# Pooling and embedding products from two-part operands in three passes, through the ring of weight slots

## What is computed

```
w in (2, 4, 8, 16):  pooled_g = window_sum_w(u_g) / min(t + 1, w) - u_g
a   = einsum("bsgc,gcd->bsgd", pooled, w_pool) * pool_scale
out = concatenate([a, gate_b * conv(gate_c * h_c)]) * silu(z)
h   = h + out @ w_out
```

```
gate = sigmoid(rmsnorm(h) @ w_ple_gate)
h    = h + (p @ w_ple_proj) * gate
```

## Time and profile before

| | |
|---|---|
| median of 3 runs | 3109.88 us |
| profiled execution's own time | 3109.86 us |
| its span | 3108.1 us |
| mean granted TensorE clock | 0.990 |
| TensorE busy | 97% |
| VectorE, ScalarE, GpSimd busy | 53%, 37%, 31% |
| 128x1024 high part, ScalarE | 279 times, mean 1058 ns |
| 128x1024 low part, GpSimd | 279 times, mean 2484 ns |

### The profile page before, as it was taken

The page is one execution under the profiler, slowest core; times in us unless marked ns, Lnnn a source line. Parts: engine busy times, 40 slices in busy tenths (PEclk is TensorE's granted clock), DMA queues, the critical chain, the costliest instruction groups (busy, mean ns, idle before and its releaser), DMA issues.

```text
span 3108.1 us, 38242 instructions
## 1 busy us (share of the span) xinstructions
PE 3014.0 (97%) x15412; PEld 2423.2 (78%) x15412; DVE 1649.9 (53%) x2710; ACT 1154.8 (37%) x1971; POOL 962.6 (31%) x700
## 2 busy tenths in 40 slices
PE   8999979999999999999999999999999999999998
PEld 7876658888878888777888866788778888888877
DVE  6989661025446564324234577767556655634436
ACT  3125553222341111113233276546445432333334
POOL 2210001232417786113531212321111133452522
PEclk9999989999999999999999999999999999999999
DMA  4110001112422333113342201331011155443323
GB/s 136 50 34 21 15 14 41 48 55 86 152 76 83 90 88 102 51 48 115 102 143 55 64 28 56 128 104 35 28 48 41 35 143 134 144 142 109 109 75 109
DMA packets 252658, 243.75 MB, mean 78 GB/s; under 512 B 15777, under 2 KB 198049, under 8 KB 251457
## 3 DMA queue, kind: packets, MB, share of 16 engines
q1 hardware_dynamic: 231536, 197.10, 21.1%
q10 hardware_dynamic: 20944, 44.21, 4.3%
HBM read 200.83 MB, written 38.73 MB: 77 GB/s over the span
## 4 chain that ended last, share of the span: by engine, by line
PE 85%; DVE 7%; ACT 4%; DMA 2%; issue 1%; POOL 1%; SPq 0%; ACTq 0%; DVEq 0%
PE psum L561 24%; PE psum L563 23%; PE psum L562 23%; PE psum L567 4%; PE psum L744 1%; PE psum L770 1%; DVE arena L2918 1%; DMA arena<-in_w_in 1%; PE psum L1205 1%; PE psum L934 1%; PE psum L879 1%; PE psum L958 1%; PE psum L750 1%; ACT WS L1221 1%; PE psum L1025 1%
## 5 line engine op out<-in xcount | busy, mean ns | idle before, releaser
L3217 POOL TENSOR_TENSOR WS<-arena,WS 128x1024 fp32r<-128x1024 f32 x279 | 691.5, 2484 | 1727.5 <-ACT WS L1221 1727.1
L561 PE MATMUL psum<-XH,WS 128*128 128x512 f32 x2600 | 1030.3, 396 | 15.0 <-ACT arena L1399 3.4
L563 PE MATMUL psum<-XH,WS 128*128 128x512 f32 x2600 | 1014.5, 390 | 0.0
L562 PE MATMUL psum<-XL,WS 128*128 128x512 f32 x2600 | 1013.7, 390 | 0.0
L561 PEld LDWEIGHTS psum<-XH,WS 128*128 128x128 f32 x2600 | 488.9, 188 | 132.5 <-issue 14.0
L563 PEld LDWEIGHTS psum<-XH,WS 128*128 128x128 f32 x2600 | 488.8, 188 | 103.5
L562 PEld LDWEIGHTS psum<-XL,WS 128*128 128x128 f32 x2600 | 489.2, 188 | 97.1 <-issue 0.7
L1221 ACT ACTIVATE WS<-arena 128x1024 fp32r<-128x1024 f32 x279 | 292.8, 1058 | 721.1 <-PE psum L563 255.4
L561 PE MATMUL psum<-WS,XH 128*128 128x512 f32 x960 | 377.9, 394 | 7.1 <-POOL WS L3217 4.9
L562 PE MATMUL psum<-WS,XH 128*128 128x512 f32 x960 | 374.3, 390 | 0.0
L563 PE MATMUL psum<-WS,XL 128*128 128x512 f32 x960 | 374.2, 390 | 0.0
(11 more groups left out here) (302 smaller groups left out, 2998.0 us busy)
## 6 DMA issues: line engine op xcount, KB each, us to landing
arena<-in_w_in SPq DMA_DIRECT2D x85, 512.0 KB, 3.8
arena<-in_w_out SPq DMA_DIRECT2D x48, 512.0 KB, 3.5
arena<-in_w_in_even SPq DMA_DIRECT2D x48, 512.0 KB, 4.0
arena<-in_w_out_even SPq DMA_DIRECT2D x32, 512.0 KB, 3.7
h_spill<-arena ACTq DMA_DIRECT2D x24, 512.0 KB, 3.1
arena<-s_table SPq DMA_DIRECT2D x8, 1536.0 KB, 6.9
arena<-in_w_in_odd SPq DMA_DIRECT2D x18, 512.0 KB, 3.8
s_table<-arena SPq DMA_DIRECT2D x32, 256.0 KB, 3.0
```

Of the source, the lines that this page charges most:

```text
L561: e.matmul(ps, wh, xh, start=start, stop=False)
L562: e.matmul(ps, wh, xl, start=False, stop=False)
L563: return e.matmul(ps, wl, xh, start=False, stop=stop)
L3217: e.tensor_tensor(lo, raw(book.raw_of.get(("w", u), 0), kbs, n), hi.bitcast(F32), SUB).then_inc(*w.up("w_lo", u))
```

## The change

Both products become `mm3` on split operands. The pooled data (two token halves of 2 x 512), the pooling weight (2 x 256), the two halves of PT3 and the two column halves of w_ple_proj become slabs of the ring. A slab whose source is on the chip (a tuple in the plan) needs no load: ScalarE waits for the events named in it and reads the tile itself. Three slabs are added behind each group's four, and four in place of the two small loads. The loops run with the token halves outermost, so VectorE's and ScalarE's evacuations take that order (PPS).

The operands' places:

```diff
-        PL, WP = view(88.75, 2, S), view(97, 2, 256)
+        PL = view(88.75, 2, S)
+        PPS = [(ch, 4 * half + j) for half in range(2) for ch in range(2) for j in range(4)]
+        def on_chip(name, half):
+            return (PL if name == "pl" else PT3)[:, :, half_of(half)]
```

TensorE's pooling product:

```diff
-                for m in range(2):
-                    for half in range(2):
+                parts = [load_w(("pl", half, ("pl2", g, 0), ("pl2", g, 1)), 2, 512) for half in range(2)]
+                u, hl = load_w(ap["w_pool_2"][256 * g:256 * g + 256, :], 2, 256)
+                for half, (v, x) in enumerate(parts):
+                    for m in range(2):
                         bank = take(pb, ("pool_ps", g, m, half), ("pool", g, m, half))
-                        w.wait_ge("wp", g)
-                        w.wait_ge("pl2", g, 0)
-                        w.wait_ge("pl2", g, 1)
+                        w.wait_ge("w_lo", v)
+                        w.wait_ge("w_lo", u)
                         for kb in range(2):
-                            t = e.matmul(psum[:, bank, :], WP[:, kb, 128 * m:128 * m + 128], PL[:, kb, half_of(half)],
-                                         start=kb == 0, stop=kb == 1)
+                            t = mm3(psum[:, bank, :], hl[0][:, kb, tile_of(m)], hl[1][:, kb, tile_of(m)], x[0][:, kb, :],
+                                    x[1][:, kb, :], kb == 0, kb == 1)
+                    ws.free()
+                ws.free()
```

TensorE's embedding product:

```diff
-            for ch in range(2):
-                r = book.raw_of.get(("ple", ch), 0)
-                wt = raw(r, 2, 512)
-                for tile in range(8):
+            parts = [load_w(("pt", half, ("pt3",)), 2, 512) for half in range(2)]
+            wts = [load_w(ap["w_ple_proj_3"][:, 512 * ch:512 * ch + 512], 2, 512) for ch in range(2)]
+            for n, (ch, tile) in enumerate(PPS):
+                (v, x), (u, hl) = parts[tile // 4], wts[ch]
+                w.wait_ge("w_lo", v)
+                w.wait_ge("w_lo", u)
+                for kb in range(2):
+                    t = mm3(psum[:, bank, :], x[0][:, kb, sl], x[1][:, kb, sl], hl[0][:, kb, :], hl[1][:, kb, :], kb == 0,
+                            kb == 1)
+                if n == 7:
+                    ws.free()
+            for _ in range(3):
+                ws.free()
```

ScalarE's `start_w` (GpSimd's is changed alike), then its program around pooling and around the embedding product. GpSimd and SyncE get the same `load` and `free` calls at the matching places:

```diff
-                w.wait_ge("raw", r)
                 if u >= 4:
                     w.wait_ge("w_used", u - 4)
-                e.activation(split_hl(u, kbs, n)[0], raw(r, kbs, n), ACT.Copy).then_inc(*w.up("w_hi", u))
+                for event in src[2:] if isinstance(src, tuple) else [("raw", r)]:
+                    w.wait_ge(*event)
+                x = on_chip(*src[0:2]) if isinstance(src, tuple) else raw(r, kbs, n)
+                e.activation(split_hl(u, kbs, n)[0], x, ACT.Copy).then_inc(*w.up("w_hi", u))
...
             for g in range(4):
-                load_wp(g)
                 run(proj_cm(2, u_ev(g)))
                 run(proj_cm(2, z_ev(2 * g)))
+                for _ in range(3):
+                    ws.load()
+                for _ in range(3):
+                    ws.free()
...
             def pps():
+                for _ in range(4):
+                    ws.load()
                 for k in range(8):
                     pp(k)
+                    if k == 3:
+                        ws.free()
                     yield
+                for _ in range(3):
+                    ws.free()
             weave((ple_norm(1), 1, True), (pps(), 1, True))
```

SyncE's `start_w`:

```diff
-                load_raw(src, kbs, n, ("w", u), ("w_lo", u))
+                if not isinstance(src, tuple):
+                    load_raw(src, kbs, n, ("w", u), ("w_lo", u))
```

More of the change, by code:

```diff
@@ L1196, in tensor_program @@
                         turn_half("ple", xs, 0)
-            for ch in range(2):
-                r = book.raw_of.get(("ple", ch), 0)
-                wt = raw(r, 2, 512)
-                for tile in range(8):
-                    bank = take(pb, ("pp_ps", ch, tile), ("pp", ch, tile))
-                    w.wait_ge("raw", r)
[L1203 to L1206, removed]
+            parts = [load_w(("pt", half, ("pt3",)), 2, 512) for half in range(2)]
+            wts = [load_w(ap["w_ple_proj_3"][:, 512 * ch:512 * ch + 512], 2, 512) for ch in range(2)]
+            for n, (ch, tile) in enumerate(PPS):
+                (v, x), (u, hl) = parts[tile // 4], wts[ch]
+                bank, sl = take(pb, ("pp_ps", ch, tile), ("pp", ch, tile)), tile_of(tile % 4)
+                w.wait_ge("w_lo", v)
[3 more added lines that the diff above has]
+                            kb == 1)
+                t.then_inc(*w.up("pp_ps", ch, tile, also=[("w_used", v)] * (n % 8 == 7) + [("w_used", u)] * (n in (11, 15))))
+                if n == 7:
+                    ws.free()
+            for _ in range(3):
+                ws.free()
             turn_half("ple", xs, 1)
@@ L1214, in start_w @@
             def start_w(u):
-                _, kbs, n = book.plan[u]
+                src, kbs, n = book.plan[u]
                 r = book.raw_of.get(("w", u), 0)
-                w.wait_ge("raw", r)
                 if u >= 4:
                     w.wait_ge("w_used", u - 4)
-                e.activation(split_hl(u, kbs, n)[0], raw(r, kbs, n), ACT.Copy).then_inc(*w.up("w_hi", u))
+                for event in src[2:] if isinstance(src, tuple) else [("raw", r)]:
+                    w.wait_ge(*event)
+                x = on_chip(*src[0:2]) if isinstance(src, tuple) else raw(r, kbs, n)
+                e.activation(split_hl(u, kbs, n)[0], x, ACT.Copy).then_inc(*w.up("w_hi", u))
             ws = Stream(book, start_w)
@@ L1590, in u_ev @@
                 return ev
[L1592 to L1598, removed]
             def s5_tables():
@@ L2727, in vector_program @@
                     split_half("ev0", lambda kb: OUT[:, 8 + kb, :], 0, range(8))
-                for m in range(2):
-                    for half in range(2):
+                for half in range(2):
+                    for m in range(2):
                         o = OUT[:, 2 * g + m, half_of(half)]
@@ L3212, in start_w @@
             def start_w(u):
-                _, kbs, n = book.plan[u]
+                src, kbs, n = book.plan[u]
                 hi, lo = split_hl(u, kbs, n)
                 w.wait_ge("w_hi", u)
-                e.tensor_tensor(lo, raw(book.raw_of.get(("w", u), 0), kbs, n), hi.bitcast(F32), SUB).then_inc(
+                x = on_chip(*src[0:2]) if isinstance(src, tuple) else raw(book.raw_of.get(("w", u), 0), kbs, n)
+                e.tensor_tensor(lo, x, hi.bitcast(F32), SUB).then_inc(
                     *w.up("w_lo", u))
@@ L3346, in gpsimd_program @@
             weave((proj_cm(28), 1, True), (s5_tables(), 1, True))
-            run(proj_cm(16))
+            for g in range(4):
+                run(proj_cm(4))
+                for _ in range(3):
+                    ws.load()
+                for _ in range(3):
+                    ws.free()
             for half in range(2):
@@ L3443, in gpsimd_program @@
             split_half("wo1", lambda kb: YT[:, kb, :], 1, (1, 5))
-            for _ in range(6):
+            for _ in range(3):
+                run(proj_th())
+            for _ in range(4):
+                ws.load()
+            for _ in range(4):
+                ws.free()
+            for _ in range(3):
                 run(proj_th())
@@ L3679, in sync_program @@
                 run(proj_th())
-            for ch in range(2):
-                load_small(("ple", ch), ap["w_ple_proj_3"][:, 512 * ch:512 * ch + 512], 2, 512)
+            for _ in range(4):
+                ws.load()
+            for _ in range(4):
+                ws.free()
             for _ in range(3):
```

6 lines of the change are left out of this document (3 added, 3 removed).

## The result

The changed kernel takes 3121.49 us (median of 5, 3119.44 to 3125.03) against 3109.88 us (3107.33 to 3112.92): 11.6 us slower, ratio 1.004, 95% interval 1.0026 to 1.0053. The forecast was 3123.5. The profiled execution has a span of 3119.0 us, 10.9 more than before.

What follows compares the result with a forecast made beforehand. TensorE, busy 3014.0 of 3108.1 us, was taken as the bound. Pooling groups 0 to 2 (+8.9), group 3 with its handover (+8.7) and the embedding (-4.1) gave +13.5 on 3109.86: 3123.5 us, range 3113 to 3129.

Steps and rivals of the forecast that it cites:

- Matmul savings: Three-pass matmuls at both products: 1.43 us saved per pooling group, 5.7 us in the embedding product, 11.4 us in all.
- The exposed weight split: Ahead of each of four pooling products, TensorE waits for the pooling weight's split, about 2.6 us idle.
- The clock term for groups 0 to 2: Behind each pooling wait of groups 0 to 2, a half-clock stretch costs 1.65 us a group.
- The row for the other side: Profile evidence against clock loss: a 2.72 us TensorE wait ending at 423.16, followed by clock 1.00.
- The clock loss of this group hides in that wait: Group 3: half clock adds nothing, since TensorE waits anyway for its first output slab's XL data.
- The blocking between VectorE and GpSimd: Group 3: VectorE's first XL part waits for GpSimd's second w_out slab; group costs 8.7 us, without blocking 6.7.
- The fifth slab: Output projection after group 3: ready 8.7 us later than today; TensorE gets there earlier and waits.
- rival 4: Half clock also behind output-projection and embedding waits, later XL parts held up repeatedly: +4 to +8, about 3129 us; chance 0.11.
- Embedding: Embedding product: a 1.6 us wait for the first weight's split against 5.7 saved, balance -4.1 us.
- Rival 1: Same waits, but the clock holds at 2.4 GHz through them: 4.95 us less, 3118.4 us; chance 0.15.
- rival 2: Group 3's handover to the output projection costs only 1.3 to 3.0 us: 3111 to 3118 us; chance 0.12.
- Rival 3: Pooling and first proj weights split before TensorE asks, no wait added, 11.4 us gained: 3098.5 us; chance 0.05.

Runs made afterwards that it cites:

- e2: The changed kernel with ScalarE issuing the pooling weight's high part one place earlier, between the last z slab's two evacuations; 3108.11 us, ratio 0.9995.
- e1: The changed kernel with its pooling parts undone on every engine, only the embedding product changed; 3103.97 us, ratio 0.9987.
- e5: The changed kernel with the embedding's slabs ordered data half 0, weight 0, data half 1, weight 1; 3120.09 us, ratio 1.0035.
- e6: The changed kernel with pooling weight one place earlier, group 3's first-half XH copies before the second w_out slab, third and fourth before h's reload; 3097.95 us, ratio 0.9961.
- e7: The changed kernel with all reorderings of e6 and the embedding's interleaved slabs of e5 together; 3094.80 us, ratio 0.9951.
- e9: The kernel before, with only the third and fourth w_out slab split ahead of the reload of h; 3104.52 us, ratio 0.9985.

## Why the prediction was right

- **Matmul savings.** 1.35 us a group at full clock (6.87 to 5.52, the restart included; forecast 1.43), 5.60 in the embedding (27.47 to 21.87; 5.71). Right.
- **The exposed weight split.** Forecast 2.6 us idle, four times 2.64 measured, and e2, which moves nothing else, takes all four away. Shown.
- **The clock term for groups 0 to 2** was mis-sized: I took 1.65 us in each of three and it came in one (group 1, 7.10 against 5.52). The two that stayed away are 3.3 us; with the waits and restarts slightly dearer than forecast, these groups were 2.9 too dear. The row for the other side was there; in the five profiles these three groups had half clock behind 5 of 15 waits, group 3 behind 5 of 5.
- **"The clock loss of this group hides in that wait"** failed. In group 3 the pooling product ran at 0.76, so it released the slot for the second output slab late: ScalarE split it at T+7.12, released by TensorE and not by the raw buffer as I had it, whose load had landed at T+6.4 (1442.62, the forecast's T+6.5), and the XH copies began at T+8.08 in place of T+7.5. At full clock the twelve matmuls of the first half would have been issued by about T+5.5 (an estimate: T+2.8 and 12 times 0.227), ahead of that load. In e2, without the wait, that split ran at T+2.9 (1429.31, with T at 1426.39).
- **The blocking between VectorE and GpSimd** was right in kind and too small: first XL part near T+11.3 (T+10.8), but the reload at T+21.3 and not T+19.7, since the six XL parts took 9.88 us. TensorE waited 4.22 for the third slab, not 3.1.
- **The fifth slab** did not hold TensorE, which I had forecast it would: its low part was written by T+38.9 (1472.68 and 2.39), but TensorE was slowed by another half-clock stretch behind the 4.22 us, which I had only in rival 4, and came to it at T+39.7. Group 3 cost 10.2 in place of 8.7, and this offsets half of what the clock term had too much.
- **Embedding** -4.0 against -4.1, with 1.44 us of waiting; e1 confirms it by time, e5 takes the wait away.
- 1.8 us of difference lies ahead of the first changed instruction, where both kernels do the same, so it says nothing about the change; nor is the 0.7 between the fifth slab and the embedding product explained.

So the forecast was 2 us off with the mechanism right and two sizes wrong in opposite directions; that it came this close is in part luck. (13.5 on 3109.86 is 3123.4; the forecast says 3123.5.) Rival 1 (the clock holds) was half true, rival 2 (a cheap handover) is refuted by group 3's 10.2 us. Rival 3 (faster) was the better kernel's story, though it needed more than it named: with the weight split before TensorE asks, e2 is only level with the kernel before, and with the handover mended as well e6 is 11.7 and e7 14.9 us faster. A part of that is clock that a shift in time gave back elsewhere: the profiles of e6 and e7 run at clock 1.00 behind the wait of 2.51 us, where the kernel before has half clock, which e9 prices at 1.6 us.

What stays open: what decides whether a wait of 2.3 to 2.7 us is followed by half clock, and why group 3's always was and group 2's never. No run here varied it.

## What to carry to other kernels

Count passes, then look at where the new operand's split stands in the issuing engine's own program. A cheaper product that needs a split behind the evacuation of the product before it waits for the whole chain (evacuation, high part, low part: 2.6 us idle here), more than the passes save (1.35 us here). In a ring with in-order engines, ask of each added slab which instruction it is queued behind and what is queued behind it; moving one issue a group by one place was worth 12 us.

## What the runs showed of the hardware

- A TensorE wait of the same length (2.64 us) was followed by a stretch at half clock in 10 of 20 cases and by full clock in the others. Group 0's wait ended between 1281.75 and 1282.41 in all five profiles, with half clock behind it in four and full clock in one. Which group it was did not fall evenly: 4, 1, 0 and 5 of five. A change in another place can so give or take 3 us (e9), so a difference of that size between two kernels needs their clocks beside it.
- VectorE's fp32 operations with two inputs in on-chip memory did not run beside GpSimd's; the two took turns. Six XL parts took 3.68 us with GpSimd quiet, 9.88 and 12.37 beside it: one of VectorE's took 1.78 in place of 0.68, and one of GpSimd's 1.74 in place of 1.27.
